# Routing stage of a GLA, Conformer and PEER layer on one Trainium2 core: the last top-16 lists of four tiles move into the stage, and the one-hots are dealt out anew

## What is computed

```
q = (x @ w_pq).reshape(N, 8, 2, 128)
s1 = einsum('nhd,kd->nhk', q[:, :, 0], k_sub1); s2 = einsum('nhd,kd->nhk', q[:, :, 1], k_sub2)
v1, i1 = top_k(s1, 16); v2, i2 = top_k(s2, 16)
cand = v1[..., :, None] + v2[..., None, :]
cidx = i1[..., :, None] * 128 + i2[..., None, :]
sc, pos = top_k(cand, 16)
idx = take_along_axis(cidx, pos); wts = softmax(sc)
out = sum over (h, e) of wts * gelu(u_exp[idx] . x) * v_exp[idx]
```

## Time and profile before

| | us |
|---|---|
| median of 3 runs | 5594.95 |
| lowest, highest | 5585.11, 5610.18 |
| profiled execution, its own time | 5575.57 |
| its span | 5574.0 |
| last score copied in mid_stage to the first instruction of route | 2949.9 to 2972.8 |
| route, to the start of experts | 2972.8 to 3210.5 |
| experts | 3210.5 to 5574.0 |

### The profile page before, as it was taken

How to read it: one execution, slowest core, us unless ns; L and a number is a source line. 1 busy time by engine, 2 the same in 40 slices (tenths; PEclk the granted TensorE clock), 3 DMA queues, 4 the chain that set the end, 5 groups by cost and what they waited for, 6 DMA issues and landing times. The chain is left out here.

```text
span 5574.0 us, 61770 instructions
## 1 busy us (share of the span) xinstructions
PE 5019.3 (90%) x23369; PEld 4097.0 (74%) x23369; DVE 3415.8 (61%) x4468; ACT 1728.7 (31%) x2276; POOL 1382.5 (25%) x1059
## 2 busy tenths in 40 slices
PE   8979999999998888989794589999999999988984
PEld 3347888888886645868684589999999898867773
DVE  7742211215676243232558968888888878878888
ACT  6743112122223111121424633333333232223332
POOL 0300000000100131000004723433434333445442
PEclk9989999999999999989897899999999999999997
DMA  9842332233333355432511699999999999999997
GB/s 362 305 163 89 101 106 92 87 103 106 116 102 113 136 201 198 156 108 91 168 38 33 149 353 381 398 375 378 375 379 387 376 374 373 391 382 408 405 410 308
DMA packets 460055, 1334.65 MB, mean 239 GB/s; under 512 B 135869, under 2 KB 193085, under 8 KB 377199
## 3 DMA queue, kind: packets, MB, share of 16 engines
q1 hardware_dynamic: 336180, 667.06, 33.8%
q0 software_dynamic: 96576, 623.69, 28.5%
q10 hardware_dynamic: 27072, 40.91, 2.1%
HBM read 1206.06 MB, written 126.56 MB: 239 GB/s over the span
## 5 line engine op out<-in xcount | busy, mean ns | idle before, releaser
L229 PE MATMUL ps<-w_hi,act_hi 128*128 128x512 f32 x3040 | 1198.4, 394 | 36.6 <-DVE w_lo L224 16.3
L231 PE MATMUL ps<-w_hi,act_lo 128*128 128x512 f32 x3040 | 1188.8, 391 | 0.0
L230 PE MATMUL ps<-w_lo,act_hi 128*128 128x512 f32 x3040 | 1188.6, 391 | 0.0
L224 DVE TENSOR_TENSOR w_lo<-w_stage,w_hi 128x2048 fp32r<-128x2048 f32 x152 | 348.1, 2291 | 1133.9 <-ACT w_hi L220 1133.0
L2421 ACT ACTIVATE x_hi<-x_stage 128x1024 fp32r<-128x1024 f32 x512 | 543.5, 1061 | 1495.9 <-DMA x_stage<-u_turned 713.5
L2501 DVE TENSOR_TENSOR x_lo<-x_stage,x_hi 128x1024 fp32r<-128x1024 f32 x512 | 625.5, 1222 | 355.8 <-ACT x_hi L2421 355.1
L2348 POOL DMA_INDIRECT u_ring<-u_exp,idx_all x256 | 598.4, 2338 | 815.9 <-DVE u_ring L2519 772.7
L2375 PE MATMUL ps<-act_hi,x_hi 128*128 128x384 f32 x2048 | 694.1, 339 | 59.8 <-DVE x_lo L2501 57.5
L2375 PE MATMUL ps<-x_hi,cx_hi 128*128 128x512 f32 x1536 | 612.2, 399 | 91.0 <-DVE cx_lo L2512 77.0
L229 PEld LDWEIGHTS ps<-w_hi,act_hi 128*128 128x128 f32 x3040 | 574.9, 189 | 161.5 <-issue 31.9
L2376 PE MATMUL ps<-act_lo,x_hi 128*128 128x384 f32 x2048 | 691.2, 338 | 0.0
(11 more groups left out here) (311 smaller groups left out, 5603.4 us busy)
## 6 DMA issues: line engine op xcount, KB each, us to landing
x_stage<-u_turned SPq DMA_DIRECT2D x256, 512.0 KB, 8.7
x_stage<-v_exp SPq DMA_DIRECT2D x256, 512.0 KB, 9.2
w_stage<-w_ada SPq DMA_DIRECT2D x96, 1024.0 KB, 6.3
w_stage<-w_in SPq DMA_DIRECT2D x96, 1024.0 KB, 5.2
d_w<-w_buf SPq DMA_DIRECT2D x6, 4096.0 KB, 20.9
gwr<-d_w SPq DMA_DIRECT2D x128, 192.0 KB, 10.6
d_gw<-gob ACTq DMA_DIRECT2D x128, 192.0 KB, 6.6
gwr<-d_gw SPq DMA_DIRECT2D x128, 192.0 KB, 10.2
```

Of the source, the lines that this page charges most:

```text
L224: dve.tensor_tensor(w_lo[:, q % 2], w_in_st[:, q], w_hi[:, q % 2].bitcast(F32), ALU.subtract).then_inc(w_split, 1)
L229: pe.matmul(out, lhs[0], rhs[0], start=first, stop=False)
L230: pe.matmul(out, lhs[0], rhs[1], start=False, stop=False)
L231: return pe.matmul(out, lhs[1], rhs[0], start=False, stop=last)
```

## The change

1. mid_stage takes only list n = 15 (tile 0) after its last product. The lists n = 16 to 19 (tiles 1 to 4) are taken in route, at the start of VectorE's round for their tile, from the same four slots of `sc`, which keep their address. The one-hots of two groups stand between the steps of such a list.
2. All first one-hots are made by VectorE (one compare of 1024 columns a group). The second go six to ScalarE, seven to GpSimd, three to VectorE out of 16. On ScalarE a second one-hot is eight Abs of 128 columns, and eight Relu of 128 columns whose scale is the negated weight and whose bias the weight of the token, both read from `id_t`; that one gets a fourth plane, the negated weights (one more ScalarE copy of 128 columns a tile).
3. PE turns the ids of tile t + 1 after group 13 of tile t, and ScalarE copies them there. ScalarE makes its one-hot for group q + 2 ahead of the takes of group q.
4. In VectorE's round the places for one-hots are spread anew (one group at each of the five places in `top16`, two at the three later ones). 14 groups of a tile stand inside the round and 2 behind it, as before.

The core of the diff:

```
-    FIRST_BY = 4 * ("act", "dve", "act", "pool")
-    SECOND_BY = 4 * ("dve", "pool", "dve", "dve")
+    SECOND_BY = ("act", "pool", "dve", "act", "pool", "act", "pool", "dve",
+                 "pool", "act", "pool", "act", "dve", "pool", "act", "pool")
+    TURN_AT = NQ - 3
...
-                for t in range(TT):
-                    lists((n_ch - 1) * TT + t)
+                lists((n_ch - 1) * TT)
...
+            turn_ids(0)
             for t in range(ND):
-                turn_ids(t)
                 for q in range(NQ):
                     spread(t, q)
+                    if q == TURN_AT and t < ND - 1:
+                        turn_ids(t + 1)
...
+            def ids(t):
+                act.wait_ge(id_ready, t + 1)
+                act.activation(id_t[:, t % 2, 3], ps[:, 5, 2 * P:3 * P], ACT.Copy, scale=-1.0)
+                act.activation(id_t[:, t % 2, 0:3].rearrange("p a n -> p (a n)"), ps[:, 5, 0:3 * P],
+                               ACT.Copy).then_inc(id_taken, 1)
...
                 act.wait_ge(s_dist, 8 * made)
-                if Q >= RING1:
-                    act.wait_ge(w_ready, 2 * (Q - RING1) + 2)
-                act.activation(one1[:, Q % RING1], dist[:], ACT.Relu, scale=-1.0, bias=1.0).then_inc(s_one1["act"], 1)
+                if Q >= RING2:
+                    act.wait_ge(w_ready, 2 * (Q - RING2) + 2)
+                for j in range(8):
+                    n = 8 * q + j
+                    made_ = act.activation(one2[:, Q % RING2, j], dist[:, j], ACT.Relu, scale=id_t[:, t % 2, 3, n:n + 1],
+                                           bias=id_t[:, t % 2, 2, n:n + 1])
+                made_.then_inc(s_one2["act"], 1)
...
+                if t > 0:
+                    slot = (late_n + t) % 4
+                    top16(4, lambda j: late_sc[:, slot, j], lambda j: top_all[:, t, late_head + j],
+                          lambda j: topi_all[t][:, late_head + j], first_hots=0)
```

More of the change, by code:

```diff
@@ L1922, in _ @@
                         lists(n + 4)
-                for t in range(TT):
-                    lists((n_ch - 1) * TT + t)
+                lists((n_ch - 1) * TT)
+        return sc, sc_at
     n_ch = D // NCOL
     project_stage("yo", a["w_gla_o"], d_m, c_o0, g_o0, gated=True, credit=True, then=a["w_out"], loaded=True)
-    mid_stage(c_o0 + n_ch, g_o0 + n_ch, c_o0 + 2 * n_ch, g_o0 + 2 * n_ch, t_groups)
+    late = mid_stage(c_o0 + n_ch, g_o0 + n_ch, c_o0 + 2 * n_ch, g_o0 + 2 * n_ch, t_groups)
     main_scope.close()
@@ L1934, in _build @@
     lk = link(None, "dve")
-    route(nc, a, stage, sem, sb, kc, ps, (idx_all, wt_all, top_all, topi_all), area, d_w, lk)
+    route(nc, a, stage, sem, sb, kc, ps, (idx_all, wt_all, top_all, topi_all, late), area, d_w, lk)
     experts(nc, a, stage, sem, sb, ps, (idx_all, wt_all), act_hi, act_lo, area, d_post, d_w, d_gw, d_f3, d_x2, d_h2)
 def route(nc, a, stage, sem, sb, kc, ps, route_sb, area, d_w, lk):
-    idx_all, wt_all, top_all, topi_all = route_sb
+    idx_all, wt_all, top_all, topi_all, (late_sc, late_at) = route_sb
+    late_head = 2 * PH - 4
+    late_n = (D // NCOL - 1) * TT
     ident = kc[:, K_ID:K_ID + P]
@@ L1948, in route, with maker @@
     RING1, RING2 = 4, 5
+    TURN_AT = NQ - 3
     half = 4 * TT * KD * P
     spare = 4 * ND * KD * P
-    FIRST_BY = 4 * ("act", "dve", "act", "pool")
-    SECOND_BY = 4 * ("dve", "pool", "dve", "dve")
-    def makers(table, Q):
-        who = table[Q % len(table)]
-        return who, sum(table[n % len(table)] == who for n in range(Q + 1))
+    SECOND_BY = ("act", "pool", "dve", "act", "pool", "act", "pool", "dve",
+                 "pool", "act", "pool", "act", "dve", "pool", "act", "pool")
+    def maker(Q):
+        who = SECOND_BY[Q % NQ]
+        return who, sum(SECOND_BY[n % NQ] == who for n in range(Q + 1))
     at_sb = nc.alloc_sbuf_tensor_at
@@ L1975, in route, with first_hot @@
         den = sb(st, "den", [P, 2, PH])
-        id_t = sb(st, "id_t", [P, 2, 3, P])
+        id_t = sb(st, "id_t", [P, 2, 4, P])
+        w_buf = sb(st, "w_buf", [P, 2, NKEY, P // 2])
+        late_end = late_at + 4 * 16 * NKEY
+        assert nc.sbuf_base <= late_at, (nc.sbuf_base, late_at)
+        sb(st, "late_room", [P, (late_end - nc.sbuf_base) // 4])
+        assert nc.sbuf_base >= late_end, (nc.sbuf_base, late_end)
         one2 = sb(st, "one2", [P, RING2, 8, P])
-        w_buf = sb(st, "w_buf", [P, 2, NKEY, P // 2])
+        sel = sb(st, "sel", [P, TT, 2, PH, TOPK])
         s_ex, s_exd, gate, route_done = sem("r_ex"), sem("r_exd"), sem("r_gate"), sem("r_done")
         id_ready, id_taken, s_dist = (sem("r_" + n) for n in ("idready", "idtaken", "dist"))
-        s_one1 = {who: sem("r_one1" + who) for who in ("act", "pool", "dve")}
-        s_one2 = {who: sem("r_one2" + who) for who in ("pool", "dve")}
+        s_one1 = sem("r_one1")
+        s_one2 = {who: sem("r_one2" + who) for who in ("act", "pool", "dve")}
         w_ready, w_taken, w_out = sem("r_wready"), sem("r_wtaken"), [sem(f"r_wout{h}") for h in range(2)]
-        def first_hot(eng, who, Q):
+        def first_hot(dve, Q):
             if Q >= RING1:
-                eng.wait_ge(w_ready, 2 * (Q - RING1) + 2)
+                dve.wait_ge(w_ready, 2 * (Q - RING1) + 2)
             t, q = divmod(Q, NQ)
[L1990 to L1998, removed]
+            dve.tensor_tensor(one1[:, Q % RING1], iota.unsqueeze(1).broadcast_to([P, 8, P]),
+                              id_t[:, t % 2, 0, 8 * q:8 * q + 8].unsqueeze(2).broadcast_to([P, 8, P]),
+                              ALU.is_equal).then_inc(s_one1, 1)
         def second_hot(eng, who, Q):
@@ L2044, in spread @@
                 Q = t * NQ + q
-                who, made = makers(FIRST_BY, Q)
-                pe.wait_ge(s_one1[who], made)
-                who, made = makers(SECOND_BY, Q)
+                pe.wait_ge(s_one1, Q + 1)
+                who, made = maker(Q)
                 pe.wait_ge(s_one2[who], made)
@@ L2075, in near @@
                 if made > 1:
-                    act.wait_ge(s_one1["act"], made - 1)
+                    act.wait_ge(s_one2["act"], made - 1)
                 for j in range(8):
@@ L2095, in _ @@
             weights(0)
+            ids(0)
             for t in range(ND):
-                act.wait_ge(id_ready, t + 1)
-                act.activation(id_t[:, t % 2].rearrange("p a n -> p (a n)"), ps[:, 5, 0:3 * P], ACT.Copy).then_inc(id_taken, 1)
                 act.wait_ge(id_taken, t + 1)
+                near(t, 0)
+                near(t, 1)
                 for q in range(NQ):
[L2101 to L2105, removed]
+                    if q + 2 < NQ:
+                        near(t, q + 2)
+                    take(t, 2 * q)
+                    take(t, 2 * q + 1)
+                    if q == 9:
                         weights(t + 1)
-                take(t, NW - 2)
-                take(t, NW - 1)
+                    if q == TURN_AT and t < ND - 1:
+                        ids(t + 1)
             weights(TT - 1)
@@ L2123, in extra, with settle, top16 @@
                         dve.wait_ge(id_taken, t + 1)
[L2124 to L2126 removed]
+                    first_hot(dve, Q)
+                    if maker(Q)[0] == "dve":
                         second_hot(dve, "dve", Q)
[L2129 to L2130 removed]
+            def settle(hots):
+                extra(hots)
                 lk.sync()
                 dve.sem_inc(gate, 1)
[L2134 removed]
+            def top16(n, values, best, where, first_hots=1):
                 for r in range(2):
                     eight = slice(8 * r, 8 * r + 8)
[L2138 removed]
+                    hots = 1 if r else first_hots
+                    settle(hots)
                     for j in range(n):
                         lk.mark(dve.max(best(j)[:, eight], values(j)))
[L2141 removed]
+                    settle(hots)
                     for j in range(n):
@@ L2144, in top16 @@
                     if r == 0:
-                        settle()
+                        settle(hots)
                         for j in range(n):
```

19 lines of the change are left out of this document (9 added, 10 removed).

## The result

| | before | with the change |
|---|---|---|
| median of 19 runs, us | 5589.19 | 5602.82 |
| lowest, highest | 5575.21, 5610.18 | 5587.02, 5616.10 |
| span of the profiled execution | 5574.0 | 5599.9 |
| route's first instruction to the first gather | 2972.80 to 3211.42 | 2952.38 to 3221.59 |
| the same, counted from the last copy of scores | 261.5 | 270.2 |

The ratio is 1.0023 with an interval of 1.0014 to 1.0032: 13 us slower (8 to 18), where 8 us faster was forecast. (The median of before is now over 19 runs; the first table's three are among them.) The stage accounts for 8.7 us of it. Where the other 5 us lie isn't shown, since the two profiled executions are 25.9 us apart and not 13. The last stage took 2362.6 us before and 2378.3 after.

What follows compares the result with a forecast made beforehand. VectorE was taken to set the routing stage, GpSimd close behind. The 21.7 us won at the start, mostly given back by GpSimd and the last write, left 8.6, rounded to 8: 5594.95 - 8 = 5587 us, range 5566 to 5605.

Steps and rivals of the forecast that it cites:

- The start: Without four lists in mid_stage, route begins at 2951.1 and not 2972.8, 21.7 us earlier; GpSimd starts at about 2981.
- VectorE's round: In route, fewer TENSOR_SCALARs, twelve more compares, one list and no id wait: 58.8 us a round, from 60.5.
- GpSimd's round: In route, seven second one-hots a tile plus the hold-up by VectorE's two-input operations: 65.2 us a tile, the deciding term.
- So ScalarE and PE hide behind GpSimd: In route's rounds, six one-hots with takes, ten plain groups and copies need 55 us a tile, below GpSimd's 65.2.
- The rival on PE's clock: PE stays at 1.2 GHz through the stage: 76 us a tile on ScalarE and PE, 20 us slower, 5615; chance 0.05.
- The ids: PE's early turn of the next tile's ids ends VectorE's 4.8 us wait over three tiles and GpSimd's some 4 a tile.
- The last rival: `id_taken` still comes late; VectorE and GpSimd wait some 4 us a tile, worth 5 to 10 us; no separate chance.
- The sum: Stage end: GpSimd ends 3176.6, last take 3180.2, VectorE 3194, last write 3201.1 against 3209.7: 8.6 us, rounded to 8.
- the write's lost slack: At the stage's end, the last `d_w` write had 4.3 us of slack; with the change it would end last, at 3201.1.

Runs made afterwards that it cites:

- e6: Kernel with the change, but four PSUM banks in turn and VectorE's compares replaced by reduces with one tensor input; stage 236.1 us against 270.2 with the change.
- e2: Kernel with the change, but PE spreads into four PSUM banks in turn, not two; stage 259.4 us against 270.2, ratio to before 0.9997.
- e4: Kernel with the change, but VectorE's compares replaced by reduces with one tensor input; stage 272.0 us against 270.2 with the change.
- e5: Kernel with the change, but PE makes 16 spare products at five of ScalarE's six one-hots a tile; stage 260.4 us against 270.2.
- e3: Kernel with the change, but ScalarE's weighted Relu is one instruction of 1024 columns with constant scale and bias; stage 261.4 us against 270.2.
- e7: Kernel with the change, but four PSUM banks and second one-hots dealt seven ScalarE, six GpSimd, three VectorE; stage 260.4 us, ratio to before 0.9988.

## Why the prediction was wrong

- **The start**: right. Route began at 2952.4 (forecast 2951.1), GpSimd at 2982.06 (2981).
- **VectorE's round, 58.8 us**: right where nothing else binds, 57.7 a tile in e6, though reduces stand there for the compares. The 2979.5 from which its three rounds were counted has no row; by the text's own terms it is 2980.5, which changes nothing.
- **GpSimd's round, 65.2 us**: right. 66.1 in tile 0, 65.9 to 67.9 in e2. A compare costs it 0.89 us (e4); 0.81 was taken. The 52.2 us that a tile was to take without harm from compares is 52.3 in e4 (156.9 / 3). The rule of the Trainium skill (GPSIMD Engine Reference, Key points) on instructions with two SBUF inputs holds: with one input at the same length the cost is gone. That GpSimd then set the round did not come true.
- **The step that failed** is "So ScalarE and PE hide behind GpSimd", 55 us a tile. It was 72, and two terms of that sum were too small. The eight Relu took 3.19 us and not 2.43, 0.76 more a one-hot, 4.6 a tile; the text had put this at 5 us and called it hidden. And the ten plain groups were priced at 0.89 us a bank, with the clock at 2.4 GHz, from two takes picked where it was high, though the same group of rows shows 1.71 after an idle stretch. By the trace after, six cycles, each of one-hot and the takes behind it, are 10.2 us each, 61 together; five of them hold two groups and the first of a tile one. The five groups more took 11 us. That makes 72.
- **The rival on PE's clock** had the right mechanism, the right sign and a price of 76 us a round, and got 0.05. It was judged by the mean clock of the rounds before, 0.81 to 0.94, and the mean fell only to 0.76 to 0.81. What decides is when the clock is low, namely at the products just after each of ScalarE's one-hots, where ScalarE waits longest for PE. That it would decide only "with the clock down for some two thirds of it" was wrong: a mean of 0.79 between 0.5 and 1 is a clock down for 42% of the time, and that was enough.
- **Why before did not show it**: its one-hots took 3.5 us on ScalarE, 2.43 + 1.06, so PE stood still for at most 2.8 us and not 5.0, the clock behind such a pause was at times high and at times low, and VectorE's 60.5 us covered the rest. The added 2.1 us a one-hot, from eight small Relus instead of one large, lengthened the pause.
- **The ids**: the early turn was to end the waits for them. GpSimd still waited 2.4 to 3.0 us a tile, some 4 before, and VectorE 12.9 us in all, more than its 4.8 before, since ScalarE's copy stands in its queue behind takes that wait for PE. The last rival had named this, with another cause.
- **The sum**: GpSimd was to end at 3176.6 and the last take at 3180.2; they ended at 3193.1 and 3198.0. The write was to end last, 7 us behind VectorE. It landed near 3218 and VectorE's last round ended at 3219.5, so the write's lost slack cost nothing by itself.

The Trainium skill has a rule for the first mis-sized term (ScalarE: Activation LUTs, What ACT_TABLE_LOAD costs): each pointer operand of an ACTIVATE adds about 93 ns. The trace agrees: the Abs have one pointer operand and the Relu two, and (3.19 - 2.43) / 8 is 95 ns for the second. For the second term the Trainium skill (TensorE: Matmul & The Clock Gate, A second HAM failure mode: psum-queue depth-cycling) describes a kernel whose products cycle through PSUM banks in bursts and lose to the clock between them. That kernel is in bf16 with 512 columns and short, frequent idles, and here it is fp32 with 128 and pauses of 4 to 5 us. The trace agrees in that the banks come up to 1.7 us apart after each pause, and by e5. Four banks, e2, were a cure for the time though not for the clock.

How much each term adds can be told from one cycle, as an estimate. It was priced at 7.8 us (4.9 + 1.07 + 1.8), with the clock kept up it is 8.8 (e5), and with the change 10.2. So the clock costs 1.4 us a cycle, some 8 a tile, and the Relu 0.7, some 4 a tile. Another 0.4 is a wait for the first bank behind the takes, 0.83 us in e5; the earlier trace rows shows it with 0.82 and the sum left it out. Together they are 15 of the 17 us that were missing. That each of the first two alone kept the round above GpSimd's 66 isn't shown: e3 and e5 each remove one of them and both end at GpSimd's bound, so they show that removing either is enough.

## What to carry to other kernels

- When work is dealt out anew, price for each engine not only its sum but its longest piece that blocks a neighbour, against the buffers between them. Two banks cover 1.8 us of PE; a piece of 5.6 us needs more banks (e2) or has to be made shorter (e3).
- With two banks a pause of PE of 4 to 5 us cost twice: the pause, and the groups after it at half the clock. Price the groups after a pause with rows that stand after a pause. With four banks the clock was as low, and GpSimd worked through two tiles without a gap all the same (e2).
- Moving a piece of serial work under a round pays only if the round's bound is another engine, and each remedy shows the next bound. Here it was the two banks, then GpSimd held up by the compares (e2), then the ids (e7). With neither banks nor compares in the way it is VectorE (e6).

## What was not expected of the hardware

- Spare products made the kernel's stage 10 us shorter at the same useful work, by PE's clock: 0.89 for 0.79 over the rounds (e5).
- A tensor_reduce over an axis of one, 128x1024, takes 1209 ns on VectorE, the two-input compare 1228, yet the first leaves GpSimd alone and the second costs it 0.89 us.
